# Stick-breaking scores as one-pass products over 128 rows of split, stacked queries and keys

## The reference, cut to what matters

```python
z = jnp.einsum('bhqd,bhkd->bhqk', qb, kb).astype(jnp.float32) * scale
mask = k_pos < q_pos
log_keep = jnp.where(mask, jax.nn.log_sigmoid(-z), 0.0)
after = lax.cumsum(log_keep, axis=3, reverse=True) - log_keep
w = jnp.where(mask, jnp.exp(jax.nn.log_sigmoid(z) + after), 0.0)
outs.append(jnp.einsum('bhqk,bhkd->bhqd', w.astype(vb.dtype), vb))
```

## Time and profile before

| | |
|---|---|
| median of 3 runs | 1062.56 us (1062.41 to 1063.36) |
| span of the profiled execution | 1061.0 us |
| PE busy | 1022.0 us, 96% |
| DVE busy | 690.2 us, 65% |
| ACT busy | 621.5 us, 59% |
| POOL busy | 126.1 us, 12% |

### The profile page before, as it was taken

How to read it: one execution, slowest core, us unless ns; L and a number is a source line. 1 busy time by engine, 2 the same in 40 slices (tenths; PEclk the granted TensorE clock), 3 DMA queues, 4 the chain that set the end, 5 groups by cost and what they waited for, 6 DMA issues and landing times. The chain is left out here.

```text
span 1061.0 us, 16887 instructions
## 1 busy us (share of the span) xinstructions
PE 1022.0 (96%) x6975; PEld 919.7 (87%) x6975; DVE 690.2 (65%) x981; ACT 621.5 (59%) x952; POOL 126.1 (12%) x119
## 2 busy tenths in 40 slices
PE   6999998999999999999999999999999989999997
PEld 5999897988998888789888799999889969899995
DVE  5788676867865687786566564545557886545554
ACT  6779676655664666375666654344456965443443
POOL 1010059440200122530000000000000100000000
PEclk9999999999999999899999999999999999999999
DMA  9885255433677432246332375565554355555540
GB/s 338 303 264 174 68 167 189 159 121 95 197 246 268 160 119 81 80 138 214 125 120 80 120 236 178 181 199 176 181 159 159 119 159 199 199 183 179 193 159 40
DMA packets 116476, 178.41 MB, mean 168 GB/s; under 512 B 5204, under 2 KB 74098, under 8 KB 116400
## 3 DMA queue, kind: packets, MB, share of 16 engines
q1 hardware_dynamic: 115136, 174.23, 50.1%
q0 software_dynamic: 1120, 2.97, 0.9%
q10 hardware_dynamic: 144, 0.13, 0.0%
HBM read 176.27 MB, written 1.05 MB: 167 GB/s over the span
## 5 line engine op out<-in xcount | busy, mean ns | idle before, releaser
L1484 DVE TENSOR_TENSOR sb_w_lo<-sb_raw,sb_w_hi 128x2048 fp32r<-128x2048 f32 (+1 forms) x139 | 309.4, 2227 | 194.3 <-ACT sb_w_hi L776 194.1
L776 ACT ACTIVATE sb_w_hi<-sb_raw 128x2048 fp32r<-128x2048 f32 (+1 forms) x134 | 254.2, 1900 | 135.4 <-PE G L2332 106.3
L2330 PE MATMUL X<-sb_hT_hi,sb_w_hi 128*128 128x256 f32 x784 | 222.9, 284 | 1.4 <-DVE sb_w_lo L1484 0.8
L2331 PE MATMUL X<-sb_hT_lo,sb_w_hi 128*128 128x256 f32 x784 | 221.3, 282 | 0.0
L2332 PE MATMUL X<-sb_hT_hi,sb_w_lo 128*128 128x256 f32 x784 | 221.2, 282 | 0.0
L2330 PEld LDWEIGHTS X<-sb_hT_hi,sb_w_hi 128*128 128x128 f32 x784 | 149.4, 190 | 3.3 <-issue 0.9
L2331 PEld LDWEIGHTS X<-sb_hT_lo,sb_w_hi 128*128 128x128 f32 x784 | 149.4, 191 | 0.7
L2332 PEld LDWEIGHTS X<-sb_hT_hi,sb_w_lo 128*128 128x128 f32 x784 | 149.4, 191 | 0.0
L2330 PE MATMUL G<-sb_w_hi,sb_uT_hi 128*128 128x512 f32 x304 | 121.0, 398 | 3.2 <-DVE sb_uT_lo L2265 1.6
L2332 PE MATMUL G<-sb_w_hi,sb_uT_lo 128*128 128x512 f32 x304 | 120.1, 395 | 0.0
L2331 PE MATMUL G<-sb_w_lo,sb_uT_hi 128*128 128x512 f32 x304 | 120.0, 395 | 0.0
(11 more groups left out here) (508 smaller groups left out, 1971.6 us busy)
## 6 DMA issues: line engine op xcount, KB each, us to landing
sb_raw<-in_mlp_w SPq DMA_DIRECT2D x64, 1024.0 KB, 5.2
sb_raw<-in_ada_w SPq DMA_DIRECT2D x22, 1024.0 KB, 5.4
sb_raw<-in_b_in_w SPq DMA_DIRECT2D x16, 1024.0 KB, 5.7
sb_raw<-in_a_in_w SPq DMA_DIRECT2D x14, 1024.0 KB, 6.6
sb_raw<-in_sb_w_qkv SPq DMA_DIRECT2D x12, 1024.0 KB, 5.1
sb_raw<-in_rg_w_in SPq DMA_DIRECT2D x8, 1024.0 KB, 5.3
sb_raw<-in_a_out_w SPq DMA_DIRECT2D x4, 1024.0 KB, 5.1
sb_raw<-in_b_out_w SPq DMA_DIRECT2D x4, 1024.0 KB, 5.3
```

Of the source, the lines that this page charges most:

```text
L776: nc.scalar.activation(split_tile(w_hi, m)[:, 0:nk * w], raw_of(b)[:, 0:nk * w], ACT.Copy).then_inc(S["w_hi"], 1)
L1484: ins = nc.vector.tensor_tensor(split_tile(w_lo, m)[:, at], raw_of(b)[:, at], split_tile(w_hi, m)[:, at].bitcast(F32), ALU.subtract)
L2330: dt32(out, lh, rh, start=first, stop=False, skip_group_check=shared)
L2331: dt32(out, lh, rl, start=False, stop=False, skip_group_check=shared)
```

## The change

Queries and keys of each head are split as the weights are. For a head, `qs_parts` has the queries' high part in the 64 rows where `qS` has the head and the queries' remainder in the other 64. `ks_hi` has the keys' high part in both halves, `ks_lo` the keys' remainder in both. Two one-pass products over 128 rows, `ks_hi` by `qs_parts` and `ks_lo` by `qs_parts`, then give all four partial products. Each of the two score products becomes two. Four sets of these tiles are used in turn.

ACT makes three copies of 64x256 for each head (`sb_high`), DVE two subtractions (`key_low`), POOL one (`sb_low`). `z_scores(h)` waits for both remainders. The tables for pieces and reads change as well, and the last read and the copies for head 12 get places of their own inside head 10.

```diff
-SB_PIECES = (3, 3, 3, 2, 2, 2, 2, 2, 2, 2, 2, 2, 2, 1, 1, 1)
+SB_PIECES = (3, 3, 3, 3, 2, 2, 2, 2, 2, 2, 2, 2, 1, 1, 1, 1)
-SB_READ = (2, 3, 9, 10)
+SB_READ = (2, 3, 8)
+SB_LAST_READ = 10
...
+            def sb_low(h):
...
+                pool.wait_ge(S["q_hi"], BH + 3 * h + 1)
+                nc.gpsimd.tensor_tensor(qs_parts[s][other, :], qS[own, h // 2, :], qs_parts[s][own, :].bitcast(F32),
+                                        ALU.subtract).then_inc(S["q_lo"], 1)
...
+            def sb_high(h):
...
+                if h % 4 == 0:
+                    act.wait_ge(S["fm_out"], 19 + h // 2 + 2)
+                if h >= S_SLOTS:
+                    act.wait_ge(S["z_head"], h - S_SLOTS + 1)
+                nc.scalar.activation(qs_parts[s][own, :], qS[own, h // 2, :], ACT.Copy).then_inc(S["q_hi"], 1)
+                for rows in (own, other):
+                    nc.scalar.activation(ks_hi[s][rows, :], kS[own, h // 2, :], ACT.Copy).then_inc(S["q_hi"], 1)
...
+            for h in range(2):
+                sb_high(h)
             split_for(first_mm["sb_v"])
...
             split_for(first_mm["sb_v"] + 1)
+            sb_high(2)
             for h in range(BH):
                 z_hi(h)
+                if h == SB_LAST_READ:
+                    sb_high(12)
                 if h + 1 < BH:
                     z_softplus(h + 1)
                 sb_weights(h)
+                if h + 3 < BH and h + 3 != 12:
+                    sb_high(h + 3)
...
+            def key_low(h):
...
+                dve.wait_ge(S["q_hi"], BH + 3 * h + 3)
+                for rows in (own, other):
+                    nc.vector.tensor_tensor(ks_lo[s][rows, :], kS[own, h // 2, :], ks_hi[s][own, :].bitcast(F32),
+                                            ALU.subtract).then_inc(S["k_lo"], 1)
+            for h in range(2):
+                key_low(h)
...
                 z_second(h)
+                if h == SB_LAST_READ:
+                    sb_read(7)
                 if h + 1 < BH:
                     z_first(h + 1)
                 z_low(h)
+                if h + 2 < BH:
+                    key_low(h + 2)
...
-                if h % 4 == 0:
-                    pe.wait_ge(S["fm_out"], 19 + h // 2 + 2)
+                pe.wait_ge(S["q_lo"], BH + h + 1)
+                pe.wait_ge(S["k_lo"], 4 + 2 * h + 2)
-                dt32(bank[:, 0:T], kS[r, h // 2, 0:P], qS[r, h // 2, :], start=True, stop=True, skip_group_check=True)
-                dt32(bank[:, T:3 * P], kS[r, h // 2, P:T], qS[r, h // 2, P:T], start=False, stop=True,
-                     skip_group_check=True)
+                for j in range(2):
+                    for part in (ks_hi[s], ks_lo[s]):
+                        dt32(bank[:, j * T:2 * P + j * P], part[:, j * P:(j + 1) * P], qs_parts[s][:, j * P:T],
+                             start=(j == 0 and part is ks_hi[s]), stop=part is ks_lo[s], skip_group_check=True)
```

More of the change, by code:

```diff
@@ L46 @@
 SB_FIRST, SB_LATER = (0, 4, 1, 5), (2, 6, 3, 7)
-SB_PIECES = (3, 3, 3, 2, 2, 2, 2, 2, 2, 2, 2, 2, 2, 1, 1, 1)
+SB_PIECES = (3, 3, 3, 3, 2, 2, 2, 2, 2, 2, 2, 2, 1, 1, 1, 1)
 SB_SPLITS = (1, 2, 4, 6, 8, 10, 12)
-SB_READ = (2, 3, 9, 10)
+SB_READ = (2, 3, 8)
+SB_LAST_READ = 10
 RAW_SLOTS, SPLIT_SLOTS = 3, 2
 Q_SLOTS = 4
+S_SLOTS = 4
 BLK = 2048
@@ L431, in build @@
                 ws = [tsb(f"ws{i}", [P, 3, P]) for i in range(2)]
+                qs_parts = [tsb(f"qs_parts{i}", [P, T], F32R) for i in range(S_SLOTS)]
+                ks_hi = [tsb(f"ks_hi{i}", [P, T], F32R) for i in range(S_SLOTS)]
+                ks_lo = [tsb(f"ks_lo{i}", [P, T], F32R) for i in range(S_SLOTS)]
             with ExitStack() as rg_stage:
@@ L741, in _ @@
                     nc.gpsimd.tensor_tensor(xn[:, t, cs], xres[:, t, cs], final_bc[:, cs], ALU.mult).then_inc(S["x_gain"], 1)
+            def sb_low(h):
+                own, other = head_rows(h)
+                s = h % S_SLOTS
+                pool.wait_ge(S["q_hi"], BH + 3 * h + 1)
+                nc.gpsimd.tensor_tensor(qs_parts[s][other, :], qS[own, h // 2, :], qs_parts[s][own, :].bitcast(F32),
+                                        ALU.subtract).then_inc(S["q_lo"], 1)
+            for h in range(BH):
+                sb_low(h)
             pool.wait_ge(S["x_ready"], XR[4])
@@ L3098, in z_scores @@
                     pe.wait_ge(S["w_exp"], h - 1)
-                if h % 4 == 0:
-                    pe.wait_ge(S["fm_out"], 19 + h // 2 + 2)
-                r = half_rows(h)
+                pe.wait_ge(S["q_lo"], BH + h + 1)
+                pe.wait_ge(S["k_lo"], 4 + 2 * h + 2)
+                s = h % S_SLOTS
                 bank = G[h % 2]
-                dt32(bank[:, 0:T], kS[r, h // 2, 0:P], qS[r, h // 2, :], start=True, stop=True, skip_group_check=True)
-                dt32(bank[:, T:3 * P], kS[r, h // 2, P:T], qS[r, h // 2, P:T], start=False, stop=True,
-                     skip_group_check=True)
+                for j in range(2):
+                    for part in (ks_hi[s], ks_lo[s]):
+                        dt32(bank[:, j * T:2 * P + j * P], part[:, j * P:(j + 1) * P], qs_parts[s][:, j * P:T],
+                             start=(j == 0 and part is ks_hi[s]), stop=part is ks_lo[s], skip_group_check=True)
                 diagonal = bank[:, 0:3 * P].rearrange("p (c n) -> p c n", c=3)[:, 0:3:2, :]
```

## The result

The kernel after took 1079.19 us in the median of 4 runs (1077.4 to 1081.95), the one before 1062.96 (1062.41 to 1064.62): a ratio of 1.0154, 95% interval 1.0137 to 1.0172. The profiled execution has a span of 1078.0 us against 1061.0. It is slower, as forecast, and by 16.2 us in the median where 12.8 were forecast.

A forecast was written before the change was run, and what follows sets the result against it. The prediction took the loop through ACT and DVE over two heads to bind, not PE: pairs of 11.81 us against 10.22, head 3 and the ends sum to +12.8 us on 1062.56, so 1075.4 us; range 1067 to 1084.

The forecast's parts named there:

- the loop of the earlier trace: Closed chain through ACT, DVE and PE over two heads: 9.68 us against PE's 10.22, so 0.54 us of slack.
- PE's gain: Scores on PE: 0.98 us a head becomes 0.59, gaining 0.39 a head, 6.2 us in 16, but lost to the loop.
- The copies and subtractions: Added to the two-head loop: ACT's copies 1.23 us and DVE's subtractions 0.90, making 11.81 us a pair, 1.59 more.
- Head 3: PE's extra piece waits for sb_read(5) ahead of z_sums(3): a PE wait of 3.0 us, offset +4.05 us.
- The forecast case: Whole kernel: loop-bound pairs of heads make it 12.8 us slower, 1075.4 us, own range 1069 to 1080; chance 0.54.
- PE's own pace again, half of 9.44: Head 4: PE runs at its own speed, -0.5 us against before, offset +3.6 in all.
- The rival of the falling clock: PE's clock halves behind waits in heads 3, 13 and 14: some 5 us more, 1080.4 us; chance 0.22.
- A granted clock under 1.00 in the stage: Sign named in advance that the forecast is wrong and PE's clock falls behind its waits.
- every wait: Reading of the skill's rule: a kernel whose PE waits once a round can lose its clock in every round.
- DVE and POOL: Rival: their subtractions delay each other, up to 0.73 us a pair, 4 us with the ends, 1079.4 us; chance 0.06.
- Hidden or half hidden: Rivals: added ACT and DVE work fits into waits, wholly 1058.1 us (chance 0.06) or half 1068.2 us (chance 0.09).
- even free copies would give only 0.54 a pair: Argument against hidden work: the two-head loop is at 9.68 us with nothing added, capping the gain at 0.54 us.

The follow-up runs named there:

- e3: e2 with ACT's copies for two heads at a time in odd heads, head 2's copies ahead of the stage, last read one head sooner: 1071.24 us.
- e4: e3 with DVE's subtractions for two heads at a time in even heads as well: 1066.88 us, 1.0041 of before.
- e8: The kernel before with three unneeded 64x256 ACT copies between weights and block in each even head from 4 on: 1069.26 us, 1.0055 of before.
- e1: The kernel after with the scores again as two float32 products, all else the same: 1081.46 us, 1.0173 of before.
- e10: The kernel after with 20 idle PE passes in head 3 ahead of the wait for sb_kS: 1077.65 us, 1.0141 of before.
- e7: The kernel before with one unneeded 64x256 ACT copy between weights and block in each even head from 4 on: 1065.89 us, 1.0026 of before.
- e2: The kernel after with the extra piece in head 4 in place of head 3: 1078.68 us, 1.0143 of before.
- e5: The kernel before with scores as three one-pass products over 64 rows, ACT copying for two heads, POOL subtracting, one piece and the last read moved: 1064.34 us.
- e9: e4 with values and reads ahead of copies and subtractions, and the keys' copy to the other 64 rows on GpSimd: 1062.3 us, 0.9994 of before.

## Why the prediction was right, and where not

**The bound.** Right. The prediction let PE's 99% of busy time stand aside for the loop of the earlier trace rows; e3 and e4 took the copies and subtractions out of the loop, and pair 12-13 fell from 12.05 to 10.73 and to 9.73, within 0.05 of the 9.68 worked out from before. e8 put three copies into before alone and lost 6.6 us.

**PE's gain.** Right in size (0.43 a head against 0.39) and right that it is lost: e1 takes it away and the end moves by 0.8 us in span, 2.3 in the medians, of 6.9.

**The copies and subtractions.** 1.18 and 0.90 us a pair measured, 1.23 and 0.90 forecast. The term that was too small is what stands around them: 0.14 and 0.12 us of later start, together 0.25 a pair. From head 5 to head 13 the offset grew by 8.1 us where 7.2 were forecast, and over heads 14 and 15 by 1.15 where it was 0.90.

**Head 3.** The mechanism and the wait were right (2.78 us against 3.0). The forecast case held the clock at full behind it, and this is the step that failed: "PE's own pace again, half of 9.44" took 6.14 us and not 4.71, and the piece of head 3, put at 1.41, took 2.73. e10, with the wait filled, has offsets of 4.43, 3.75 and 4.78 at heads 3 to 5, against 4.05, 3.6 and 4.7 forecast. So of the 4.2 us that the forecast lacks in the profiled execution (17.0 less 12.8; 3.4 in the medians) 3.0 are the clock, and the rest is what e10 still has over the forecast: 0.1 up to head 5, 0.9 from there to head 13, 0.25 at the end.

**The rival of the falling clock** gave 2.4 us for this place, near the 3.0 measured, and 1 to 1.5 behind each of two more waits. Behind the wait of 2.73 us at `z_sums(13)` the clock did fall, and the windows of after show it:

```profile
595.00:600.00 5.00, 3.78 (x15) 3.56 (x16) 4.27 (x6) 2.06 (x5) 0.00 (x0) 0.66 0.00 0
```

It cost next to nothing, for at `z_sums(14)` PE still waited 0.72 us for DVE: of the wait of 2.3 us that the prediction had there, the slower passes filled the rest. The 1 to 1.5 us that the rival charged there were too much, since what PE loses behind one wait comes off the next one. A granted clock under 1.00 in the stage, the prediction's own sign for this rival, did come. So the likeliest case and this rival each were half of the truth, and the time, 1079.2, lies between their 1075.4 and 1080.4. The rule of the Trainium skill that the prediction set beside this rival ("TensorE: Matmul & The Clock Gate", "HAM oscillation — how this bites in real kernels") holds here only in part: after waited 12 times for `sb_es_lo`, some 0.9 and 1.5 us in turn and once 1.94, and from 540 to 595 us its clock stood at 1.00. That section of the Trainium skill tells of one kernel with longer waits, for transfers, than any in this stage, so the prediction's "every wait" is more than it says.

**DVE and POOL.** The other rival didn't come in the loop. POOL's subtraction in odd heads started beside DVE's block and took 2.08 us, in even ones 0.73:

```profile
554.74 0.73 POOL L753 TENSOR_TENSOR sb_qs_parts<-sb_qS,sb_qs_parts 64x256 fp32r<-64x256 f32 x1 [3.83 <-ACT sb_qs_parts L1319]
560.90 2.08 POOL L753 TENSOR_TENSOR sb_qs_parts<-sb_qS,sb_qs_parts 64x256 fp32r<-64x256 f32 x1 [5.43 <-ACT sb_qs_parts L1319]
```

DVE's block beside it kept its 2.29 us, and `z_low` its 0.56, so within the heads POOL paid, as the prediction said. Ahead of the stage it was the other way round once: POOL's subtraction had been running since 497.93, for 2.54 us, when DVE's first one for the keys started at 499.80, and that took 0.95 us where 0.42 is usual.

**Hidden or half hidden.** Out by e8, for the copies. But one sentence of the prediction was too generous: "even free copies would give only 0.54 a pair" took the slack as one sum over the loop, and e7 shows that PE's sums cut the loop in two, with 0.25 us in the half that the copies are in. It made no difference here, with both halves over PE's time.

## What to carry over

Where one engine is at 99%, close the loop that the others run through before taking work off it: if that loop is nearly as long, the gain is capped by its slack, and what the change adds to it counts in full. Work out the slack between each two points at which the bound engine takes part, not over a whole round, for it can't be carried past them. And a wait that is put into the bound engine's stream can cost more than itself, where the clock falls behind it and no later wait takes up the loss: 3.0 us behind the wait of head 3, nothing behind that of head 13. The traces with and without idle passes in that wait differ by these 3.0 us, the medians by 1.5 with intervals that overlap.

## What the runs showed of the hardware

- The granted clock fell to 0.50 behind PE waits of 2.78 and 2.73 us (after), 2.61 and 2.35 (e1), 2.72 (e10), 2.18 (e3), and 1.16 and 0.84 us close together (e2), each time for some 3 to 7 us. It stayed at 1.00 behind single waits of 0.85 (e3), 1.71 (e4) and 1.94 us (after), and where 20 passes filled the 2.78 us (e10).
- Behind a wait the first pass of `z_sums` has its successor after 0.28 us, without a wait after 0.17 (550.19 in e7, 549.59 in before).
- One-pass products over 64 rows, three for each block, took as long as the float32 product that they replace: 0.88 against 0.89 us for 256 and 128 columns (e5). The stacked passes over 128 rows took 0.46 (after).
- Small copies on ACT follow each other after 0.31 us where they write the same rows (three in 1.02 us in e8) and after 0.43 where the second writes other rows than the first (0.84 for two of 0.41 in after, at 554.57).
- A GpSimd copy of 64x256 took 0.40 us, and 2.38 where it started just behind DVE's block (e9); its subtraction of the same shape 0.73, and 2.08 beside DVE's block. Where GpSimd had started first, DVE's subtraction of 64x256 took 0.95 us instead of 0.42 (after, at 499.80).
